# Expert blocks of 64 rows with one shared overflow pair, in a hybrid SSD and mixture-of-experts decoder step

## The reference, cut to what matters

```
g_sel = argmax(t @ w_rg + b_rg)                  # one of 4 groups
top_v, top_i = top_k(softmax(le[g_sel]), 2)      # two of its 8 experts
for g in range(N_EGROUPS):
    a = jnp.einsum('td,edf->tef', t, w_gate[g])
    up = jnp.einsum('td,edf->tef', t, w_up[g])
    act = jax.nn.silu(a) * up * gate[:, g, :, None]
    out = out + jnp.einsum('tef,efd->td', act, w_down[g])
```

## Time and profile before

| | us |
|---|---|
| median of 3 runs | 1385.13 |
| the profiled execution | 1385.16 |
| its span, first to last instruction | 1383.4 |
| TensorE busy | 1292.4 (93%) |
| VectorE, GpSimd, ScalarE busy | 559.7, 500.3, 403.8 |

### The profile page before, as it was taken

The page is one execution under the profiler, slowest core; times in us unless marked ns, Lnnn a source line. Parts: engine busy times, 40 slices in busy tenths (PEclk is TensorE's granted clock), DMA queues, the critical chain, the costliest instruction groups (busy, mean ns, idle before and its releaser), DMA issues.

```text
span 1383.4 us, 24222 instructions
## 1 busy us (share of the span) xinstructions
PE 1292.4 (93%) x9611; PEld 1040.4 (75%) x9611; DVE 559.7 (40%) x794; ACT 403.8 (29%) x602; POOL 500.3 (36%) x387
## 2 busy tenths in 40 slices
PE   4999999999998998899899899999989999999992
PEld 4999999999866975887697599999986444444430
DVE  5444523004554956575495571023443121211112
ACT  4121125333324333442443361132234111111102
POOL 5344432343433534352354444334312222222320
PEclk7999999999999999999999999999999999999996
DMA  5232322225204510720352032444536999999964
GB/s 149 71 82 76 78 62 66 83 76 133 67 1 116 137 31 19 187 63 16 101 138 61 19 112 77 101 134 138 192 155 246 372 372 361 360 368 366 379 206 149
DMA packets 187366, 204.71 MB, mean 148 GB/s; under 512 B 15096, under 2 KB 164728, under 8 KB 179025
## 3 DMA queue, kind: packets, MB, share of 16 engines
q1 hardware_dynamic: 176258, 189.96, 42.0%
q0 software_dynamic: 8192, 9.83, 3.1%
q10 hardware_dynamic: 2824, 3.56, 0.7%
HBM read 188.93 MB, written 29.72 MB: 158 GB/s over the span
## 4 chain that ended last, share of the span: by engine, by line
PE 76%; DVE 10%; issue 5%; ACT 4%; DMA 4%; SPq 1%; DVEq 1%; ACTq 0%; POOLq 0%; POOL 0%
PE acc L618 37%; PE pTS L1024 8%; PE pTS L1037 4%; PE acc L1061 4%; DVE area L1245 4%; PE acc L881 4%; PE pTS L1071 2%; PE pTS L730 2%; DMA ring<-in_w_in 2%; PE pTS L788 1%; PE pY L782 1%; PE pY L806 1%; PE acc L971 1%; DVE big L1307 1%; PE pY L978 1%
## 5 line engine op out<-in xcount | busy, mean ns | idle before, releaser
L618 PE MATMUL acc<-h_parts,ring_parts 128*128 128x328 f32 (+1 forms) x3840 | 547.2, 304 | 21.7 <-issue 7.5
L618 PEld LDWEIGHTS acc<-h_parts,ring_parts 128*128 128x128 f32 x3840 | 532.9, 190 | 38.1 <-issue 37.9
L1850 POOL TENSOR_TENSOR ring_parts<-ring,ring_parts 128x1024 fp32r<-128x1024 f32 x112 | 283.8, 2534 | 462.0 <-ACT ring_parts L1559 462.0
L1559 ACT ACTIVATE ring_parts<-ring 128x1024 fp32r<-128x1024 f32 x112 | 118.4, 1058 | 414.6 <-PE acc L618 367.4
L2022 POOL DMA_INDIRECT y_sum<-big,area x32 | 50.6, 1582 | 203.0 <-DMA y_sum<-big,area 176.2
L1024 PE MATMUL pTS<-area,big 128*64 128x512 f32 x384 | 113.3, 595 | 0.2 <-ACT big L1778 0.2
L618 PE MATMUL acc<-u_parts,ring_parts 128*128 128x264 f32 (+1 forms) x640 | 109.4, 299 | 0.0
L618 PEld LDWEIGHTS acc<-u_parts,ring_parts 128*128 128x128 f32 x640 | 96.4, 188 | 0.0
L1245 DVE SCALAR_TENSOR_TENSOR area<-area,xvec 128x616 f32<-128x616 f32 x72 | 90.1, 1252 | 10.5 <-DVE area L1243 0.6
L1024 PEld LDWEIGHTS pTS<-area,big 128*64 128x64 f32 x384 | 34.9, 137 | 76.4 <-issue 76.4
L618 PE MATMUL acc<-area_parts,ring_parts 128*128 128x264 f32 (+1 forms) x512 | 91.1, 299 | 0.0
(11 more groups left out here) (342 smaller groups left out, 1612.1 us busy)
## 6 DMA issues: line engine op xcount, KB each, us to landing
ring<-in_w_in SPq DMA_DIRECT2D x80, 512.0 KB, 4.0
area<-in_w_gate SPq DMA_DIRECT2D x24, 1024.0 KB
area<-in_w_up SPq DMA_DIRECT2D x24, 1024.0 KB
area<-in_w_down SPq DMA_DIRECT2D x24, 1024.0 KB, 10.6
area<-in_state_ssm SPq DMA_DIRECT2D x16, 512.0 KB, 6.9
out<-area SPq DMA_DIRECT2D x16, 512.0 KB, 6.7
ring<-in_w_ssd_out SPq DMA_DIRECT2D x16, 512.0 KB, 4.2
ring<-in_w_gate SPq DMA_DIRECT2D x8, 1024.0 KB
```

Source lines behind the costliest of these rows:

```text
L618: m = nc.tensor.matmul(acc[a][:, h, 0:n], w[s][:, k, :], x[:, k, h * HALF:h * HALF + n], start=first and k == 0 and w is w_hi and x is hi, ...
L1559: a_.activation(w_hi[b % 2], w_raw[b % 2], ACT.Copy).then_inc(hi_done, 1)
L1850: gp.tensor_tensor(w_lo[b % 2], w_raw[b % 2], w_hi[b % 2].bitcast(F32), ALU.subtract).then_inc(lo_done, 1)
```

## The change

Every expert has 64 places in its pair (`CAP = 64`), and the overflow part of each pair goes: its gather, transposes, products, evictions and scatter. A 17th pair takes places 64 to 127 of the two experts with the most rows. VectorE picks these after pair 0 (`pick_units`), finds their rows after pair 2 (`unit_slots`), TensorE turns them into columns in pair 4, and VectorE writes the indices after pair 6 (`unit_rows`). SP reads the two expert numbers into registers and loads their weights once more. The 17th pair scatters twice, its low and its high half, since both experts may hold the same row. The conditional rounds (now for more than 64 rows in a third expert, or more than 128 in one) have blocks of 96 (`LATER`), and their slots are computed after pair 8 (`later_slots`).

Gate and up become two products with 256 columns each, into two banks, each with its own semaphore for its weights, and SP loads gate of both experts, then up, then down, each as soon as TensorE has left that part of the slot. The first three experts' parts come in that order too, and expert 3 is loaded as soon as the output projection has ended. The histories are turned one step a pair in pairs 8 to 15, copied by ScalarE to a row buffer, and stored by two transfers of ScalarE's queue.

```diff
-CAP = 96
-ROUNDS = -(-(T - CAP) // CAP)
-SLOTS = CAP * (1 + ROUNDS)
+CAP = 64
+LATER = 96
+ROUNDS = -(-(T - CAP) // LATER)
+SLOTS = CAP + ROUNDS * LATER
 EPS = 1e-6
 TAIL = XH * (1 + NSEQ)
 STAIL = SH * (1 + NSEQ)
 BLK = 8 * P
 PAIRS, MAIN = NE // 2, 64
-OVER = CAP - MAIN
+UNITS = 2
 DUMP, NO_TOKEN = T, 2048
+assert SLOTS % CAP == 0 and ROUNDS * LATER % CAP == 0
 UNROLL = 4
+TAIL_PAIR = 8
...
-            def load_gate_up(n):
-                for part, w in zip(wexp[n % 4][0:2], (wg, wu)):
-                    sp.dma_start(part, w[expert_of(n)]).then_inc(gu_in[n // 2 % 2], 16)
-
-            def load_down(n):
-                sp.dma_start(wexp[n % 4][2], wd[expert_of(n)]).then_inc(dn_in[n // 2 % 2], 16)
-
...
+            def load_part(part, n, e=None):
+
+                w, done = (wg, wu, wd)[part], (gw_in, uw_in, dn_in)[part]
+                src = w[expert_of(n)] if e is None else w[bass.ds(e, 1)].rearrange("o p k f -> (o p) k f")
+                sp.dma_start(wexp[n % 4][part], src).then_inc(done[n // 2 % 2], 16)
...
+                    load_part((f - 2) // 2, f % 2)
             sp.wait_ge(x_t, 8)
-            load_gate_up(2)
-            load_down(2)
+            for part in range(3):
+                load_part(part, 2)
+            sp.wait_ge(w_done, wo_at(7)[0] + 2)
+            for part in range(3):
+                load_part(part, 3)
...
-            sp.wait_ge(s_tl, 8)
-            sp.dma_start(outs[3][0, 0], tails[0:XH, 0:CONV]).then_inc(tails_out, 16)
-            sp.dma_start(outs[6][0].rearrange("b r c -> (b r) c"), tails[XH:TAIL, 0:CONV]).then_inc(tails_out, 16)
-            sp.dma_start(outs[4][0, 0], tails[0:SH, CONV:]).then_inc(tails_out, 16)
-            sp.dma_start(outs[7][0].rearrange("b r c -> (b r) c"), tails[SH:STAIL, CONV:]).then_inc(tails_out, 16)
-            sp.wait_ge(tails_out, 16 * 4)
-            load_gate_up(3)
-            load_down(3)
-            for p in range(2, PAIRS):
-                sp.wait_ge(m_gu, 2 * (p - 2) + 2)
-                load_gate_up(2 * p)
-                load_gate_up(2 * p + 1)
-                sp.wait_ge(m_dn, 2 * (p - 2) + 2)
-                load_down(2 * p)
-                load_down(2 * p + 1)
-
-            for s in range(2):
-                sp.wait_ge(ye_out[s], 32 * PAIRS // 2)
+            for p in range(2, PAIRS + 1):
+                last = p == PAIRS
+                if last:
+                    sp.wait_ge(r_unit, 1)
+                    units = [sp.value_load(uid[0:1, u:u + 1], min_val=0, max_val=NE - 1) for u in range(UNITS)]
+                for part in range(3):
+                    if part < 2:
+                        sp.wait_ge(m_gu, 2 * (p - 2) + part + 1)
+                    else:
+                        sp.wait_ge(m_dn, p - 1)
+                    for j in range(2):
+                        load_part(part, 2 * p + j, units[j] if last else None)
+
+            sp.wait_ge(ye_out[0], 16 * (PAIRS // 2 + UNITS))
+            sp.wait_ge(ye_out[1], 16 * (PAIRS // 2))
...
             turn_main(0)
-            pe.wait_ge(r_ids, 3)
-            turn_over(0)
-            pe.wait_ge(s_tl, 8)
-            for p in range(PAIRS):
+            for p in range(PAIRS + 1):
                 xT_ = pair_xT[p % 2]
-                pe.wait_ge(gu_in[p % 2], 64 * (p // 2 + 1))
-                pe.wait_ge(m_xe, 2 * p + 1)
+                for part, w_in in ((0, gw_in), (1, uw_in)):
+                    pe.wait_ge(w_in[p % 2], 32 * (p // 2 + 1))
+                    if part == 0:
+                        pe.wait_ge(m_xe, p + 1)
+                        if p >= 1:
+                            pe.wait_ge(m_act, p)
+                    for k in range(8):
+                        for j in range(2):
+                            m = nc.tensor.matmul((pT, pS)[part][main_of(j), 0:FE], xT_[:, k, main_of(j)],
+                                                 wexp[(2 * p + j) % 4][part][:, k, :], start=k == 0, stop=k == 7)
+                    m.then_inc(m_gu, 1)
+                if p < PAIRS:
+                    turn_main(p + 1)
+
+                pe.wait_ge(m_act, p + 1)
                 if p >= 1:
...
+                    pe.wait_ge(m_hc, p)
                 for ft in range(FK):
                     m = nc.tensor.transpose(pO[:, ft * P:(ft + 1) * P], h_main[:, ft * P:(ft + 1) * P], ident[:, :])
                 m.then_inc(m_ht, 1)
...
+                if p >= TAIL_PAIR and p < TAIL_PAIR + 8:
+                    tail_rows(p - TAIL_PAIR)
+                if p == 4:
+                    pe.wait_ge(r_unit, 2)
+                    for n in range(2 * TILES):
+                        r = ROWS[n % TILES]
+                        m = nc.tensor.matmul(pY[:, 0:2], at_unit[0:r, n, :], u_of[0:r, n, :], start=n == 0, stop=n == 2 * TILES - 1)
+                    m.then_inc(r_gs, 1)
+
+                pe.wait_ge(dn_in[p % 2], 32 * (p // 2 + 1))
+                pe.wait_ge(m_hc, p + 1)
+                if p == 0:
+                    pe.wait_ge(r_gs, 2)
+                else:
+                    pe.wait_ge(m_ye, p)
+                for h in range(2):
                     for ft in range(FK):
...
+                        for j in range(2):
+                            m = nc.tensor.matmul(acc[1][main_of(j), h, :], hT_main[:, ft, main_of(j)],
                                                  wexp[(2 * p + j) % 4][2][:, ft, h * 512:(h + 1) * 512],
                                                  start=ft == 0, stop=ft == FK - 1)
...
+                m.then_inc(m_dn, 1)
...
+            def pick_units():
+
+                link(v.tensor_copy(u_count, pY[:, 192:192 + NE]))
+                for u in range(UNITS):
+                    link(v.tensor_reduce(u_best[:, u:u + 1], u_count, AX.X, ALU.max))
+                    link(v.tensor_scalar(u_tmp, u_count, u_best[:, u:u + 1], None, ALU.is_equal))
+                    link(v.scalar_tensor_tensor(u_tmp, eoff, float(CAP), u_tmp, ALU.add, ALU.mult))
+                    link(v.tensor_reduce(u_at[:, u:u + 1], u_tmp, AX.X, ALU.max))
+                    link(v.tensor_scalar(u_oh[:, u, :], u_tmp, u_at[:, u:u + 1], None, ALU.is_equal))
+                    link(v.scalar_tensor_tensor(u_count, u_oh[:, u, :], -1e6, u_count, ALU.mult, ALU.add))
...
+
+            def unit_slots():
+
+                for n, m_ in enumerate((m1_, m2_)):
+                    at, has = at2[n], u_has[:, n, :]
+                    link(v.tensor_scalar(fits, at, float(CAP), None, ALU.is_lt))
+                    link(v.tensor_copy(has, fits))
+                    for u in range(UNITS):
+                        link(v.tensor_tensor(p3, m_.rearrange(fl), u_oh[:, u:u + 1, :].broadcast_to([P, TILES, NE]), ALU.mult))
+                        link(v.tensor_reduce(u_in, p3, AX.X, ALU.add))
+                        link(v.scalar_tensor_tensor(t_, u_in, float(2 * NO_TOKEN), at, ALU.mult, ALU.add))
+                        link(v.tensor_scalar(t_, t_, float(-2 * NO_TOKEN - MAIN), None, ALU.add))
+                        for i in range(TILES):
+                            x = v.tensor_scalar(at_unit[:, n * TILES + i, u * MAIN:(u + 1) * MAIN], places, t_[:, i:i + 1], None,
+                                                ALU.is_equal)
+                        link(x)
+                        link(v.tensor_scalar(ec, at, float(CAP + MAIN), None, ALU.is_lt))
+                        link(v.tensor_tensor(ec, ec, u_in, ALU.mult))
+                        link(v.tensor_tensor(has, has, ec, ALU.max))
+                    v.tensor_copy(u_of[:, n * TILES:(n + 1) * TILES, 0], tokback)
+                    x = v.tensor_copy(u_of[:, n * TILES:(n + 1) * TILES, 1], gate[:, n, :])
+                x.then_inc(r_unit, 1)
+
+            def unit_rows():
+
...
+            for p in range(PAIRS + 1):
+                dve.wait_ge(m_silu, p + 1)
+                dve.wait_ge(m_gu, 2 * p + 2)
+                v.tensor_tensor(h_main, g_main, pS[:, 0:FE], ALU.mult).then_inc(m_act, 1)
+                dve.wait_ge(m_ht, p + 1)
                 v.tensor_copy(hT_main.rearrange("p a b -> p (a b)"), pO[:, 0:2 * P]).then_inc(m_hc, 1)
...
                 if p >= 2:
-                    dve.wait_ge(ye_out[p % 2], 32 * (p // 2))
-                results = [(ye_main[p % 2], acc[1].rearrange("p a b -> p (a b)"), gate_main), (ye_over[p % 2], pS[:, :], gate_over)]
-                for n, (to, of, by) in enumerate(results if p < PAIRS - 1 else results[::-1]):
-                    dve.wait_ge(m_dn, 2 * p + n + 1)
-                    v.tensor_scalar(to, of, by[:, p:p + 1], None, ALU.mult).then_inc(m_ye, 1)
+                    dve.wait_ge(ye_out[p % 2], 16 * (p // 2))
+                if p == PAIRS:
+                    dve.wait_ge(r_unit, 3)
+                dve.wait_ge(m_dn, p + 1)
+                v.tensor_scalar(ye_main[p % 2], acc[1].rearrange("p a b -> p (a b)"), gate_main[:, p:p + 1], None, ALU.mult
+                                ).then_inc(m_ye, 1)
+                if p == 0:
+                    pick_units()
```

(38 more changed lines are left out.)

323 lines of the change are left out of this document (123 added, 200 removed).

## The result

The changed kernel took 1376.51 us (median of 4 runs, 1375.76 to 1377.92) against 1385.28 for the kernel before on the same chip: a ratio of 0.9931, interval 0.9916 to 0.9946. The gain is 8.8 us where 21.2 were forecast. The profiled execution has a span of 1376.2 us against 1383.4.

A forecast was written before the change was run, and what follows sets the result against it. Transfers were to bound the loop at 18.0 us a pair: loop start 1061.0 + 270 + down 3.6 + VectorE 2.0 + scatters 8.0 + end 17.5 = 1362.1 span, plus 1.76 gives 1363.9 us; range 1350 to 1378.

The forecast's parts named there:

- Part 1: Expert pairs on TensorE: without the overflow work a pair needs 12.9 us instead of 18.82.
- Part 2: Expert loop: transfers become the bound, weights 15.85 us plus row gathers and scatters 2.3, taken as 18.0 us per pair.
- The forecast's own sign of trouble: Expert loop: a pair period over 18.8 us, as slow as now, would show the forecast wrong.
- The lower end of the forecast's period: Expert loop: 17.2 us per pair, if half the row transfers' time goes (1.27 us off), less 2%.
- Rival A: Expert loop: transfers stay at today's 18.8 us a pair, the last 3% being gaps any order has; 1376 us, chance 0.16.
- Part 3: The added 17th pair: costs one more transfer period, 18.0 us, not TensorE's 12.9.
- Part 4: Weight loads: pair 2's can be issued 3.6 us into pair 0 instead of 11.8; then the queue runs without a break.
- Part 5 (c): Before the loop: expert 3's earlier loads delay the writes of h2 rows; +2.5 us, between 0 and about 4.
- Part 6: Work put into the pairs: histories and VectorE's small operations are hidden or covered by queued loads, 0 us.
- Part 7: The end: after the last load TensorE needs 3.6 us, VectorE and hand-over 2.0, two nearly empty scatters 8.0.
- Rival D: Expert loop: waits drop TensorE's clock to 1.2 GHz, 25.2 us a pair, some 1514 us; decides from 19.4; chance 0.05.
- A clock below 0.9 in the loop: Expert loop: TensorE's granted clock under 0.9, listed as a sign of being wrong; 1.00 was expected.

The follow-up runs named there:

- e11: Changed kernel with only the slot order altered, so that consecutive rows of an expert go to different groups of four partitions; 1366.32 us, ratio 0.9875.
- e13: Kernel before the change, with e11's slot order for the first 64 slots of each expert; 1385.65 us, ratio 0.9998.
- e4: Changed kernel without the 17th pair: its weights, products, gather and second scatter left out; 1354.57 us, ratio 0.9774.
- e2: Changed kernel with expert 3's three loads issued only after the writes of h2 rows have landed; 1375.47 us, ratio 0.9927.
- e8: Changed kernel with expert 3's gate and up loads behind the writes of h2 rows, its down load behind the first gather; 1373.97 us, ratio 0.9911.
- e6: Changed kernel with all scatters bounded to row 0, so the experts' results are missing from the sum; 1337.61 us, ratio 0.9652.

## Why the prediction was right and where it was wrong

The mechanism held in its main line: TensorE's relief is worth only what the transfers allow. The sizes did not, and the forecast was 12.6 us low. In the terms of its own sum, the span is 14.1 us late: 5.6 in the start of the loop's transfers (1066.6 against 1061.0), 5.1 in 15 periods of 18.34 instead of 18.0, and 3.4 behind the last load. By its parts:

**Part 1 held.** The 64 records take 6.91 us in the second pair and the down product 3.65; the whole pair, 1074.26 to 1086.69, is 12.4 us on TensorE with the 0.56 us wait (12.9 forecast).

**Part 2 is the step that failed, and not by its mean.** Weights take 87.6% of 260 us for 92.94 MB, 2.45 us per MB or 15.4 a pair (15.85 forecast); rows take 12.9%, 33.5 us for 14 gathers and 15 scatters, 2.3 a pair (2.3 forecast). The sum is 17.7 where I took 18.0. What was wrong is that I worked with the mean of 16 engines. The last load landed at 1341.62, when about one engine in 16 was still busy (share 0.07), and the fall from 1322 on says that the others had run ahead by up to 20 us. So the mean share reads 1.0 until 1322 and hides the engine that is behind. The 105 rows of the fullest engine against 74 in the mean are 31 x 0.49 = 15 us over the loop; 11.5 show as the missing share at the end. e11 took 18 of the 31 rows away, and the weights landed 7.0 to 7.9 us earlier. The kernel before could not show this: TensorE gave every engine time to catch up, and e13 shows no gain from the other order. The forecast's own sign of trouble, a period over 18.8, didn't come either: 15 periods of (1341.66 - 1066.6) / 15 = 18.3. (The lower end of the forecast's period, 17.2, is the 17.12 without the 2% that the text says is taken off; with it the end would be 16.8.)

Rival A gave 1376, the right time for a wrong reason: its gaps "that any order has" are not there (the share is 1.0), and part of the lateness goes away with another order of slots.

**Part 3 held.** The 17th pair costs a transfer period: 18.1 us by e4.

**Part 4 held in the loop, not at its start.** The loads of pair 2 were issued at 1065.32, 6.0 us into pair 0 instead of 3.6, because the gate half ran at the lower clock.

**Part 5 (c) was undersized, and this is the second step that failed.** The write of h2 rows took 8.17 us under the loads of expert 3, 5.5 more than before, where I took 2.5 and had 4 as the upper end. e2 gave the 2.65 back by moving those loads. I did not price a second effect at all. After the long wait TensorE was granted 0.73 and then 0.70 in two windows of 15 us, and the first pair's products took 9.45 us instead of 6.9. Together the start of the loop's transfers was some 5.6 us late (1065.32 against 1059.7). But e2 and e8 show that to start the first pair earlier gives back little (1.0 and 2.2 us) as long as the loads only change places; the clock of that pair stayed low in both.

**Part 6, half right.** VectorE's 56 small operations did delay the transposes of pair 3, the fourth (one wait of 5.7 us for L1479), and nothing followed, as forecast. The histories were put at 0 and cost 0 to 3.

**Part 7 held but for the clock.** Two nearly empty scatters took 8.35 us (8.0 forecast). The last down product, after TensorE had mostly waited, was granted 0.50, 1.2 GHz, and took 6.48 us: +2.9. Rival D named this. In the loop (1075 to 1341) the mean clock was 0.95, with short stretches below, such as 0.57 in 1306 to 1310, that the waits for transfers hide; it cost 2.5 and 2.9 us at the two ends. A clock below 0.9 in the loop was on the list of signs of being wrong, and it came without setting the pace. Nor would D have needed 19.4 us a pair to decide: by its own figures TensorE sets the pace from the 18.0 us of the transfers on.

The account of the span by causes: 5.6 (start) + 11.5 (uneven engines) + 2.9 (last product) + 0.6 (tail) = 20.6, less 6.4 by which the mean work of the 15 pairs was overestimated, (1341.66 - 11.5 - 1066.6) / 15 = 17.57 a pair against 18.0. That is 14.2; the difference of 1376.2 and 1362.1 is 14.1. The 6.4 is the remainder and was not measured by itself, though the 17.7 above is near it. The parts don't say what their removal would give back: e8 moved the start by 5.5 us and gained 2.2.

## What to carry to other kernels

When a change moves the bound to the transfers, ask for the fullest transfer engine, not for the mean share: rows gathered or scattered into low slots first pile up on the same few of them, and another pattern of one iota took 7 to 8.6 us off. A long fall of the transfer share behind a full stretch, here 20 us with 11.5 missing, was its sign. And loads that are moved out of a critical stretch are not gone: where transfers are short, they only wait elsewhere.

## What the hardware showed that I had not expected

- The order of rows over partitions moves the last weights: with 87, 105 and 127 rows on the fullest engine, if each group of four partitions has its engine, they landed at 309.9, 317 and 329.8 us; part of the last figure has another cause.
- A 512 KB write of rows took 2.65 us alone and 8.17 beside 3.1 MB of queued loads.
- The packet of a scattered, accumulated row of 4 KB takes 327 ns, that of a gathered one 159 (medians).
- With a full queue the handing over of two 1 MB loads held SP for 8.17 us, and a load landed 28 us after its issue.
- One core moved 413 GB/s over 225 us (e6), and 392 with rows among the weights.
